# The 16 query slabs as whole 32-bit products, with the scaling of the input on GpSimd and its split at the end of the routing

## What is computed

```python
hf = h.reshape(t, d)                       # h = rmsnorm(x, norm_ffn_g)
q = (hf @ w_query).reshape(t, PEER_HEADS, 2, PEER_HALF)
s1 = jnp.einsum('thc,hnc->thn', q[:, :, 0], keys1)
s2 = jnp.einsum('thc,hnc->thn', q[:, :, 1], keys2)
v1, i1 = lax.top_k(s1, PEER_TOPK)
v2, i2 = lax.top_k(s2, PEER_TOPK)
...                                        # the 16 best sums of pairs, their experts idx, softmax gate
act = jax.nn.gelu(jnp.einsum('thkd,td->thk', expert_u[ib], hb), approximate=False)
return jnp.einsum('thk,thkd->td', gb * act, expert_v[ib])
```

## Time and profile before

| what | value |
|---|---|
| median of 3 runs | 2117.55 us |
| the profiled execution, its own time | 2116.37 us |
| its span, first to last instruction | 2114.6 us |
| mean granted TensorE clock | 0.987 |
| TensorE (PE) busy | 2041.4 us, 97% |
| DVE busy | 1443.1 us, 68% |
| ACT busy | 1057.8 us, 50% |
| GpSimd (POOL) busy | 59.8 us, 3% |
| loads from HBM | 348.77 MB, 167 GB/s over the span |

### The profile page before, as it was taken

How to read it: one execution, slowest core, us unless ns; L and a number is a source line. 1 busy time by engine, 2 the same in 40 slices (tenths; PEclk the granted TensorE clock), 3 DMA queues, 4 the chain that set the end, 5 groups by cost and what they waited for, 6 DMA issues and landing times.

```text
span 2114.6 us, 40945 instructions
## 1 busy us (share of the span) xinstructions
PE 2041.4 (97%) x15332; PEld 1943.2 (92%) x15332; DVE 1443.1 (68%) x2353; ACT 1057.8 (50%) x1642; POOL 59.8 (3%) x40
## 2 busy tenths in 40 slices
PE   7999899999999999999999999899999999999997
PEld 7989898989999999999879999799999999999997
DVE  5877898866666666666776556765557556956555
ACT  5444537854444444444455445644445444645443
POOL 0000430000000000000000000000000000000000
PEclk9999999999999999999999999999999999999999
DMA  6435542145555555555665555345555555435553
GB/s 206 130 127 163 209 140 83 48 150 188 188 182 190 183 189 188 183 190 182 208 199 179 185 183 171 104 159 179 183 184 170 182 186 169 160 127 176 182 181 99
DMA packets 101456, 353.60 MB, mean 167 GB/s; under 512 B 11392, under 2 KB 16640, under 8 KB 101120
## 3 DMA queue, kind: packets, MB, share of 16 engines
q1 hardware_dynamic: 100944, 350.13, 51.2%
q10 hardware_dynamic: 432, 2.36, 0.3%
HBM read 348.77 MB, written 3.67 MB: 167 GB/s over the span
## 4 chain that ended last, share of the span: by engine, by line
PE 87%; DVE 7%; ACT 4%; issue 1%; DMA 0%; SPq 0%; DVEq 0%; ACTq 0%
PE front L1802 39%; PE acc L1802 33%; PE tile L1802 15%; DVE w_lo L1099 1%; ACT w_hi L686 1%; DVE chosen L1538 0%; DVE rstd L1122 0%; DVE cand L1481 0%; DVE orr L1391 0%; ACT G L880 0%; PE front L2281 0%; DVE S L1325 0%; ACT h_hi L705 0%; DVE h L1142 0%; ACT picks_raw L874 0%
## 5 line engine op out<-in xcount | busy, mean ns | idle before, releaser
L1099 DVE TENSOR_TENSOR w_lo<-raw,w_hi 128x1024 fp32r<-128x1024 f32 x616 | 753.7, 1224 | 162.4 <-ACT w_hi L686 161.9
L686 ACT CAST w_hi<-raw 128x1024 fp32r<-128x1024 f32 x632 | 659.6, 1044 | 313.8 <-PE front L1802 144.3
L1802 PE MATMUL front<-h_hi,w_hi 128*128 128x256 f32 x2272 | 644.9, 285 | 6.9 <-ACT h_hi L705 5.5
L1802 PE MATMUL front<-h_hi,w_lo 128*128 128x256 f32 x2272 | 643.6, 284 | 0.0
L1802 PE MATMUL front<-h_lo,w_hi 128*128 128x256 f32 x2272 | 633.8, 283 | 0.0
L1802 PEld LDWEIGHTS front<-h_hi,w_hi 128*128 128x128 f32 x2272 | 438.3, 193 | 12.8 <-ACT h_hi L705 4.8
L1802 PEld LDWEIGHTS front<-h_hi,w_lo 128*128 128x128 f32 x2272 | 438.4, 193 | 0.0
L1802 PEld LDWEIGHTS front<-h_lo,w_hi 128*128 128x128 f32 x2272 | 432.1, 192 | 4.2
L735 ACT ACTIVATE scaled<-scaled 128x256 f32<-128x256 f32 x196 | 81.9, 418 | 460.5 <-DVE scaled L1185 248.9
L1180 DVE TENSOR_TENSOR scaled<-front,rstd 128x512 f32<-128x512 f32 x88 | 60.9, 691 | 275.9 <-PE front L1802 275.7
L1802 PE MATMUL tile<-h_hi,w_hi 128*128 128x256 f32 x704 | 204.9, 293 | 10.6 <-DVE h_lo L1243 4.9
(11 more groups left out here) (284 smaller groups left out, 2798.3 us busy)
## 6 DMA issues: line engine op xcount, KB each, us to landing
raw<-stream SPq DMA_DIRECT2D x632, 512.0 KB, 3.7
early_u<-stream SPq DMA_DIRECT2D x20, 512.0 KB, 3.7
early_activations<-early_out SPq DMA_DIRECT2D x20, 128.0 KB, 3.5
scaled<-early_activations SPq DMA_DIRECT2D x10, 128.0 KB, 3.6
x<-x_t SPq DMA_DIRECT2D x2, 512.0 KB, 4.5
keysT<-keys_t ACTq DMA_DIRECT2D x1, 1024.0 KB, 6.3
attc<-attention_constants ACTq DMA_DIRECT2D x1, 1024.0 KB, 5.5
out_t<-h SPq DMA_DIRECT2D x4, 256.0 KB, 2.2
```

The source lines that it names most:

```text
L686: nc.scalar.copy(w_hi[:, s, :], raw[:, s, :]).then_inc(hi_ready, 1)
L1099: nc.vector.tensor_tensor(w_lo[:, s, :], raw[:, s, :], w_hi[:, s, :].bitcast(F32), ALU.subtract).then_inc(lo_ready, 1)
L1802: return nc.tensor.matmul(out, lhsT, rhs, start=start, stop=stop, **kw)
```

## The change

- The 16 query slabs are multiplied whole: 8 products of 32-bit `raw` with 32-bit `h32` = x times gain, which ACT makes where it made h_hi. TensorE waits for `landed`, and for each of the first 8 pieces of h32. No part of a query slab is split; ACT, DVE and GpSimd only raise the counts.
- A query slab's place in the ring is free when its products are done (`slab_used`), so the loads of slabs 4 to 15 and of the first four expert slabs wait for that, and SP issues each one slab group (4) later in its list.
- ACT no longer makes h_scaled: GpSimd makes it from h32 and rstd, in 4 operations before its first split. GpSimd splits the low parts of the first 4 expert slabs only.
- h_hi is made by ACT after query tile 11, h_lo by DVE behind the last chosen rows, ahead of its wait for the picks. TensorE waits for all of h_lo ahead of the expert steps.

```diff
--- before.py
+++ after.py
@@ -590,10 +590,12 @@
             sp.wait_ge(slab_used, first["branch"] + 1)
             for j in range(U_BUFFERS):
                 load_early(j)
-            steady(n, n + 2 * RING)
+            for m in range(n, n + RING):
+                load(m)
             for i in range(16):
-                if n + i + 2 * RING < first["peer"] + RING:
-                    load(n + i + 2 * RING)
+                m = n + RING + i
+                sp.wait_ge(slab_used, m + 1 - RING)
+                sp.dma_start(raw[:, m % RING, :], stream[m, :, :]).then_inc(landed[m % RING], 16)
                 if i in EARLY_AT:
                     store_early(EARLY_AT[i])
             for j in range(len(EARLY_AT), EARLY):
@@ -637,20 +639,21 @@
             for q in range(1, N_NORMS):
                 if q == 2:
 
+                    pool.wait_ge(rstd_ready, 2)
+                    pool.wait_ge(h_gained, KT)
+                    for k in range(0, KT, 2):
+                        nc.gpsimd.tensor_tensor(h_scaled[:, k:k + 2, :], h32[:, k:k + 2, :],
+                                                rstd[:, :].unsqueeze(1).broadcast_to([P, 2, T]),
+                                                ALU.mult).then_inc(h_scaled_steps, 1)
                     for n in range(first["wquery"] + RING, first["peer"] + RING):
-
                         pool.wait_ge(lo_ready, n)
                         pool.wait_ge(hi_ready, n + 1)
-                        nc.gpsimd.tensor_tensor(w_lo[:, n % RING, :], raw[:, n % RING, :],
-                                                w_hi[:, n % RING, :].bitcast(F32),
-                                                ALU.subtract).then_inc(lo_ready, 1)
-                        k = 2 * (n - first["wquery"] - RING)
-                        if k < KT:
-                            pool.wait_ge(rstd_ready, 2)
-                            pool.wait_ge(h_gained, k + 2)
-                            nc.gpsimd.tensor_tensor(h_scaled[:, k:k + 2, :], h_scaled[:, k:k + 2, :],
-                                                    rstd[:, :].unsqueeze(1).broadcast_to([P, 2, T]),
-                                                    ALU.mult).then_inc(h_scaled_steps, 1)
+                        if n < first["peer"]:
+                            pool.sem_inc(lo_ready, 1)
+                        else:
+                            nc.gpsimd.tensor_tensor(w_lo[:, n % RING, :], raw[:, n % RING, :],
+                                                    w_hi[:, n % RING, :].bitcast(F32),
+                                                    ALU.subtract).then_inc(lo_ready, 1)
                 for k in range(0, KT // 2, 2):
                     wait_x(pool, q, k + 1)
                     if k == 0:
@@ -673,6 +676,10 @@
             def split_hi(n, turn=None, per=0):
 
                 if turn is None and n >= NSLAB:
+                    return
+                if turn is None and first.get("wquery", NSLAB) <= n < first.get("peer", NSLAB):
+                    act.wait_ge(hi_ready, n)
+                    act.sem_inc(hi_ready, 1)
                     return
                 s = n % RING
                 loads = n // RING + 1
@@ -829,7 +836,11 @@
             if "peer" in first:
 
                 nc.scalar.dma_start(keysT[:, :, :], keys_in).then_inc(keys_in_sem, 16)
-                operand_hi(1, "norm_ffn_g")
+                for k in range(KT):
+                    wait_x(act, 1, k)
+                    g = COL["norm_ffn_g"] + k
+                    nc.scalar.activation(h32[:, k, :], x[:, k, :], ACT.Copy,
+                                         scale=cols[:, g:g + 1]).then_inc(h_gained, 1)
                 square_last(1)
                 split_hi(late)
                 n = first["wquery"]
@@ -847,14 +858,12 @@
                     if i == 1:
                         root(1)
                         split_hi(n + RING)
-                        for k in range(KT):
-                            g = COL["norm_ffn_g"] + k
-                            nc.scalar.activation(h_scaled[:, k, :], x[:, k, :], ACT.Copy,
-                                                 scale=cols[:, g:g + 1]).then_inc(h_gained, 1)
                     if i >= 1:
                         split_hi(n + i + RING)
                     if i in EARLY_AT:
                         early_gelu(EARLY_AT[i])
+                    if i == 11:
+                        operand_hi(1, "norm_ffn_g")
                 for j in range(len(EARLY_AT), len(EARLY_AT) + EARLY_AT_END):
                     early_gelu(j)
                 act.wait_ge(gate_diff, 1)
@@ -1094,6 +1103,11 @@
 
                 if turn is None and n >= NSLAB:
                     return
+                if turn is None and first.get("wquery", NSLAB) <= n < first.get("peer", NSLAB):
+                    dve.wait_ge(lo_ready, n)
+                    dve.wait_ge(hi_ready, n + 1)
+                    dve.sem_inc(lo_ready, 1)
+                    return
                 s = n % RING
                 dve.wait_ge(hi_ready, n + 1 if turn is None else turn * per + (n + 1))
                 nc.vector.tensor_tensor(w_lo[:, s, :], raw[:, s, :], w_hi[:, s, :].bitcast(F32),
@@ -1423,7 +1437,6 @@
                     split_lo(n + m + RING)
             late = n + 7 + RING
             if "peer" in first:
-                operand_lo(1, "norm_ffn_g")
                 add_squares(1)
                 split_lo(late)
 
@@ -1547,6 +1560,7 @@
                                                 gsum[:, :, :, 1:2].broadcast_to([P, TT, HEADS, TOPK]),
                                                 ALU.mult).then_inc(picks_ready, 1)
 
+                operand_lo(1, "norm_ffn_g")
                 dve.wait_ge(picks_copied, 2)
 
                 def rows(t, b):
@@ -2106,7 +2120,15 @@
                     ins.then_inc(keys_done, 1)
 
                 for i in range(16):
-                    project("wquery", i, n + i, h_hi, h_lo, 8 if i == 0 else None)
+                    j = tile_at["wquery"] + i
+                    free_tile(j)
+                    slot = (n + i) % RING
+                    pe.wait_ge(landed[slot], 16 * ((n + i) // RING + 1))
+                    for k in range(KT):
+                        if i == 0:
+                            pe.wait_ge(h_gained, k + 1)
+                        ins = mm(tile_buf(j), raw[:, slot, k * P:(k + 1) * P], h32[:, k, :], k == 0, k == KT - 1)
+                    ins.then_inc(slab_used, 1)
                     if i == 1:
                         norm(1)
                         pe.wait_ge(keys_in_sem, 16)
@@ -2164,6 +2186,7 @@
                         elif 1 <= 4 * late_turn + b <= KT:
                             seed_x(4 * late_turn + b - 1)
                 pe.wait_ge(g_copied, T // 4)
+                pe.wait_ge(nh_lo, 2 * KT)
                 mlp(first["peer"], LOOP_STEPS, 1, 0, True, 0, more=EARLY)
                 pe.wait_ge(eye_ready, 1)
                 for tt in range(TT):
```

## The result

| | before | after |
|---|---|---|
| median (16 runs each) | 2117.55 us (2115.07 to 2118.98) | 2120.86 us (2118.91 to 2123.90) |
| ratio to before, 95% interval | | 1.0019 (1.0012 to 1.0026) |
| profiled execution, span | 2116.37, 2114.6 us | 2119.48, 2117.7 us |
| its mean granted clock | 0.987 | 0.991 |
| GpSimd busy | 59.8 us | 31.1 us |

The kernel became 3.3 us (0.16%) slower. 2121.0 was forecast, within 2117.5 to 2125.0. The interval excludes no change, but the difference lies under the 4.2 us that the forecast counted as no change.

What follows compares the result with a forecast made beforehand. TensorE, 87% of the chain, was taken as the bound. Stage end 2.1, low part 2.2, less 0.9 at the picks gave +3.4, rounded to +3.5: 2121.0 us median, range 2121 - 3.5 to 2121 + 4.

Steps and rivals of the forecast that it cites:

- Whole products: Query slabs on TensorE: 8 whole products take 3.46 us against 2.87 split, 0.59 more per slab, 9.4 us for 16.
- The rival with the ratio of four to three: Query slabs: a whole-product slab takes 3.83 us, +5.9 in all, 2126.9 us; chance 0.05.
- Start: First query products: TensorE waits only for ACT's h32, starts at 231.1 instead of 231.65 us; two slabs end at 238.05.
- The 3.8 us wait goes: Query stage: TensorE's 3.8 us wait for DVE to free a key-score bank disappears, as GpSimd's query splits are gone.
- The end of the stage: Last top-k search, best_keys(15), starts at 308.05 us, +1.8; with a 0.3 us collision, +2.1 at the first chosen row.
- The low part: Before the picks: DVE's eight h_lo operations take 3.28 us, 1.11 of it formerly idle, so pick rows come 2.17 us later.
- Given back at the picks: First block of picks: ACT's gating no longer starts late behind its table load, -0.9 us.
- Clock: TensorE's wait before the picks grows to some 3.8 us; granted clock taken as unchanged, with 1.7 us possible either way.
- The rival of a second slow stretch: Behind the longer wait for the picks: a second low-clock stretch, +1.7, 2122.7 us; chance 0.37 together with a DVE collision.
- A shift that grows after 440 us: Past the picks: named as a sign of being wrong; everything from the picks on should shift by one amount.
- faster by DVE's pace: Slabs 8 to 15: DVE's top-k sets the pace, best_keys(15) 5.8 us earlier, time 4.5 lower, 2113.0 us; chance 0.06.
- The change doesn't do what it says: Query stage and routing's end: operand split already hidden, only +1.3 left, 2118.9 us; chance within the no-change case.

Runs made afterwards that it cites:

- e4: Kernel before, with GpSimd's 12 splits of query slabs left out (old data as low parts, same number of products): 2112.21 us, ratio 0.9971.
- e1: Changed kernel, with h_hi made by ACT after tile 2 and h_lo by GpSimd behind its scalings, none on DVE: 2118.10 us, ratio 1.0006 to before.
- e2: Changed kernel, with DVE's eight h_lo operations done twice in the same place: 2123.17 us, ratio 1.0033 to before.
- e8: Changed kernel, with 8 unused whole products put in front of TensorE's wait for the picks: 2119.66 us, ratio 1.0018 to before.
- e9: Kernel before, with 4 unused whole products in front of TensorE's wait for the picks: 2114.84 us, ratio 0.9991.
- e5: Changed kernel, with only query slabs 0 to 7 whole, the rest split, h_lo on GpSimd ahead of its scalings: 2114.54 us, ratio 0.9992 to before.
- e6: Changed kernel, with only query slabs 0 to 5 whole, the rest split, h_lo on GpSimd: 2116.71 us, ratio 0.9998 to before.
- e7: Changed kernel, with only query slabs 0 to 3 whole, the rest split, h_lo on GpSimd: 2123.65 us, ratio 1.0031 to before.
- e3: Changed kernel, with 7 of the 8 whole products per query slab (last 128 features left out of the queries): 2116.55 us, ratio 0.9994 to before.
- e10: Changed kernel, with only the first 8 slabs whole, h_lo on GpSimd, and 4 unused products in the wait for the picks: 2112.88 us, ratio 0.9982 to before.

## Why the prediction was right, and where it was not

**Whole products: right.** 3.46 us each, as the early slabs showed, a ratio of 1.21 to a split slab. The rival with the ratio of four to three would have made it 3.83; it is out.

**Start: right.** h32 from ACT lets TensorE start at 231.25 for 231.65, two slabs end at 238.39 (238.05 predicted, and this execution entered the stage 0.12 later; the rest is that the two took 7.14 us and not 6.92). The loads and ACT's new place for h_hi cost nothing, as said: TensorE's only wait from 229 to 310 us is the first, 1.1 us for h32.

**The 3.8 us wait goes: right,** with its cause as named, GpSimd's splits beside DVE's candidates. e4 shows it alone.

**The end of the stage: the step that failed.** I put search 15 at 308.05, behind the last key scores at 307.95. Those were done at about 308.2 (started 307.75, 0.44 us), so TensorE's part was nearly right. But search 15 came at 308.62, because it hangs on the key scores of slab 13 (done at 300.57): behind them DVE has 7.96 us of work in a row (search 13, a step of sums, search 14), TensorE only 7.6 until the last scores. The same chain existed before, from key scores 13, done at 297.53. Chain of work, then DVE in order of time, kernel before:

```profile
297.07 0.46 PE front L1802 x4
```

```profile
297.62 0.50 DVE L1442 MAX8 top_v<-front 128x8 f32<-128x128 f32 x2 [0.82 <-PE front L1802]
...
300.12 1.16 DVE L1481 TENSOR_TENSOR cand<-top_v 128x128 f32<-128x128 f32 x2
```

It had a collision of 0.7 in it (candidates 1.16 for 0.46). So +3.0 of TensorE less 0.7 makes +2.3. The slip stands in the prediction's own times: it has DVE at search 14 at about 298, before the scores of slab 13 can be there (300.57 here); search 14 came at 306.24. I had reckoned on +1.8 and on 0.3 of collision at the last candidates; they start 0.17 us behind the last split's end and take 0.46. Two errors of 0.6 and 0.3 stand against each other, and the first chosen row came 2.35 later for the predicted 2.1: that this term came out so near is luck.

**The low part: right.** Directly behind the chosen rows, 3.25 us, first pick row at 331.68 (331 to 332 predicted), of which 2.0 remain after the 1.11 us that DVE waited before; e1 and e2 show that nothing hides it.

**Given back at the picks: half the size.** With the table load out of the way I took 0.9 off; at equal clock e8 has 105.84 and e9 106.29 us from the pick row to the first expert slab: 0.45.

**Clock: taken as unchanged, true of the profiled execution.** In the profile of after there is one stretch, as before. But the last column shows three outcomes for this wait: no stretch (106.3 in e1 and e5), the usual one (107.95 before, e4, e6 and e7), and a longer one. With the table in place the three are 105.84 (e8), 107.51 (after) and 108.77 (e3): the usual stretch costs 1.7 us, the longer one 2.9. The rival of a second slow stretch put its time at 2122.7, and that is the mean of the upper group; the lower one has 2119.5. The longer stretch would make 1.3 of the 3.3 between them, a first expert slab at 1.2 GHz, as before had it, 1.5 more. There is a third place: the kernels whose profiled execution has a mean clock of 0.987 or 0.988 (before, e4, e6) stand at 1.2 GHz for some 10 us around 1100 to 1115 us, the kernel after for 3.4, and seven of the eight runs of the upper group have that mean clock, those of the lower 0.990 or 0.991. No execution of the upper group was profiled, so what it is made of is not shown, nor is what makes the clock differ around 1100 us.

**Sum.** At equal clock 3.75 us at the first expert slab, from e8 and e9, where 3.4 had been added up: 2.2 at the stage's end, 2.0 for the low part, less 0.45. That the medians then differ by 3.3 us, beside a forecast of 3.5, is in part luck: where the clock falls moves an execution by 1.5 us and more at the first expert slab alone, and the median of the kernel after falls in the gap between its two groups. A shift that grows after 440 us was named as a sign of being wrong. It does grow, from 2.4 us behind the first expert slab to 3.1 at the end, by way of 1.5, and what it follows there is not shown. The rivals: *faster by DVE's pace* fell, since TensorE sets when key scores 13 are there, and e3 shows that it pays to take products away. *The change doesn't do what it says* fell with e1 and e2: but for the 1.11 us in which DVE waited before, the 3.25 us hide nowhere. What the change wins is real: without GpSimd's collisions e4 has search 15 at 71.7 us. The kernel after, without them too, has it at 78.0: of 9.4 us more on TensorE 6.3 came through, more than the 4.1 won. Then come 2.0 for a low part put where nothing hides it.

**Not tried:** h_lo on DVE in its idle time during the query stage, other places for the early expert slabs, and the low parts of the expert slabs on another engine.

## What to carry to other kernels

Before adding up a stage's end, find the last point where the engine that finishes it really waited; the end moves with that event, here the scores of slab 13 and not the last ones. When two ways of computing differ in which engine they load, mix them by position: here whole products where the other engines are behind, split products where TensorE is, and neither pure form was the best (e10 beside e8 and e9, with h_lo moved as well). Check what GpSimd reads beside DVE additions of two tensors, and look for waits of TensorE that unused products on data at hand can fill.

## What the runs showed of the hardware beyond the expected

- Equal waits, unequal clock: 1.69 us of TensorE's waiting in front of the picks brought a stretch at 1.2 GHz in the kernel before, e4, e6 and e7 and none in e1 and e5, in one execution of each. The 3.66 us of the kernel after brought 3.4 us of it, the 3.65 us of e3 6.8 us.
- The first expert slab, too, ran at 1.2 GHz in some executions (4.64 to 4.66 us: before, e4, e5, e6) and at 2.4 GHz in the others (3.14 to 3.16 us). Whether these 1.5 us make much of the spread of a kernel's runs (2.0 us in e8, 8.2 in e4) is not shown.
- DVE and GpSimd can fall in step: in e7 the collisions recur at each step, and search 15 comes 6.3 us later than in the kernel before, though GpSimd has the same 16 splits, and the four operations of h_lo besides.
